# Two gate tiles of layer 0 are computed during the context's latent attention group instead of after it

## The chip, the cores and the metric

The kernel runs on one core of a Trainium2 chip. The metric is the device time of one execution in microseconds (us). Its engines are called by name here and by their short names in the profile: TensorE (PE, with PEld for its weight loads), VectorE (DVE), ScalarE (ACT), GpSimd (POOL) and SyncE (SP), which issues most DMAs. TensorE writes to eight PSUM banks; everything else lies in SBUF.

## The reference, cut to what matters

Two blocks with two layers each follow one another. The first is an image transformer block over 256 latent tokens and 256 context tokens of width 1024, the second a hybrid of retention, state space, stick-breaking and memory attention. The change lies in layer 0 of the first block. There, for the latent and for the context tokens:

```python
p = h @ w_in                       # h (tokens, 1024): normed and modulated input
gate_logits = p[..., :2048]        # two gates of 1024 columns
...
y_mla = dense_attention(mq, [mk_c, mk], [mv_c, mv])       # 8 heads, latent attention
y_na = neighborhood_attention(nq, nk, nv, nk_c, nv_c, rpb)  # 8 heads, with a bias
g = sigmoid(gate_logits)
y = g[..., :D_MODEL] * (y_mla @ w_mla_o) + g[..., D_MODEL:] * (y_na @ w_na_o)
x = x + gt1 * (y @ w_out)
```

In layer 0 the context tokens attend too (256 queries over 256 keys, without the bias); the latent tokens attend over 512 keys. All in float32.

## The kernel before

Activations lie transposed: 1024 features are eight k-steps of 128 partitions, and the 512 tokens (256 context, 256 latent) are columns. A product that must be exact to float32 is split: an operand is a high part (ScalarE copies it into a rounded type) and a low part (VectorE subtracts), and one k-step of a tile is three matmuls, high weight by high input, high by low, low by high (`split_product`, lines 562 to 565). A gate tile is 128 of the 1024 columns of the first gate for all 512 tokens: eight k-steps, 24 matmuls of 128x512. There are eight of them, called g1 0 to 7.

Weights come in chunks in the order of their use. A chunk of the large kind holds two gate tiles. It lands in one of three ring slots and is split into one of two buffers, `w_parts[0]` and `w_parts[1]`, in turn. `w_parts[1]` lies over the tensor `h`, where the low parts of the layer's input lie at first (`h_lo1`). Before it can be used, VectorE copies the low parts into `h_parts` (line 2315), eight copies, two a turn.

Attention runs in *turns*, one for each head and half of the queries: in layer 0 four groups of 16, `mla` (turns 0 to 15, latent queries, 512 keys), `mlac` (16 to 31, context queries, 256 keys: the context's latent group), `nac` (32 to 47, context, neighbourhood heads) and `na` (48 to 63, with the bias). Three engines walk through the same list, each at its own pace, and meet at semaphores:

- TensorE (`softmax_attention`, line 681) in turn i: the score product of turn i (line 906; in the last two groups those of turns i and i+1 together in even turns), the transposition of the probabilities of turn i-3 (line 715), a part of a value product of a unit of four turns, in odd turns (line 914), and then `fill(i)`, which is `gate_step` (line 931). Scores and transpositions share five banks in rotation, value products have one, gate tiles two.
- VectorE (`softmax`, line 1886) in turn i: the maximum of turn i's scores (line 1898; in `na` the bias before it), the reciprocal and the scaling for turn i-1 (lines 1902, 1904), every fourth turn the copy of a value product out of its bank (line 2299), and then `with_tile` (line 2301): the low-part copies in turns 32 to 35, and halves of weight splits (line 1941).
- ScalarE (`softmax`, line 1359) in turn i: the copy of the transposed probabilities of turn i-3 (line 1372), the exponential of turn i (line 1378), and then `split_gate` (line 1596): halves of weight splits (line 1423) and the exponential of a finished gate tile (line 1611).

Which turn does which gate work is set by constants. `gate_step` starts at turn `FILL_FROM[0]` = 34 and does two k-steps (6 matmuls) a turn, a tile in `FILL_STEPS[0]` = 4 turns: tiles 0 to 7 fill turns 34 to 65. `split_turn` (line 500) puts the halves of the four later weight chunks at turns 36, 37, then 44, 45, then 52, 53 and 60, 61 of ScalarE, and one turn later on VectorE. VectorE's first half waits for both of ScalarE's. The first chunk (tiles 0 and 1) is split in turns 4, 8, 11 and 13 of the first group. Behind the turns, TensorE goes on with the second gate and the output products (`turn_tile`), all of them split products.

Layer 1 has no context queries, two groups, and its own constants (18 and 2).

Of the kernel before, what the change touches and what calls it, by code (L numbers as in the profile page):

```python
# [41 lines left out]
KT = D // P  # L42
# [12 lines left out]
VALUES_AT = (2, 4, 7)  # L55
LINE = 128
TURN_BANKS, VALUE_BANKS, GATE_BANKS = (0, 1, 2, 3, 4), (5,), (6, 7)
FILL_FROM, FILL_STEPS = (34, 18), (4, 2)
GATES = [4, 5, 6, 7, 0, 1, 2, 3] + list(range(8, 16))
ADA = 24  # L60
FIRST = 8
# [198 lines left out]
def program(nc, dram, numbers):  # L260
# [3 lines left out]
    with ctx:  # L264
# [5 lines left out]
        def sem(name):  # L270
            if name not in sems:
                sems[name] = ctx.enter_context(nc.semaphore(name))
                count[name] = 0
            return sems[name]
# [9 lines left out]
        def event(name, *key):  # L284

            assert not numbers or (name, *key) in numbers, (name, *key)
            return sem(name), numbers.get((name, *key), 1)
# [20 lines left out]
        def given(ring_name, key):  # L308
            return rings[ring_name][numbers.get(("slot", ring_name, key), 0)]
# [46 lines left out]
        def part(name, shape, at):  # L356
            return nc.alloc_sbuf_tensor_at(name, shape, F32R, offset=at)
# [8 lines left out]
        h_lo1 = part("h_lo1", [P, KT, TT], h_at)  # L366
# [71 lines left out]
        at = 2048 + 8 * T  # L438
# [57 lines left out]
        def tile_index(l, g, u):  # L496

            return 16 * [t[0] for t in groups(l)].index(g[0]) + u

        def split_turn(l, i):  # L500


            out = []
            for c in range(1, 5):
                key = ("g1", l, 2 * c) if c < 4 else ("g2", l, 0)
                for a in range(2):
                    turn_of = FILL_FROM[l] + 2 * FILL_STEPS[l] * (c - 1) + 2 - l + a
                    if i == min(turn_of, 16 * len(groups(l)) - 1):
                        out.append((place[key][0], a))
            return out  # L510
# [5 lines left out]
        def groups(l):  # L516


            mla = lambda hd: (hd, slice(0, QK))
            na = lambda hd: (hd // 2, slice(ND * (hd % 2), ND * (hd % 2) + ND))  # L520
            out = [("mla", mq, mk, mv, mla, TC, 4, 0)]
            if l == 0:
                out.append(("mlac", mq, mk, mv, mla, 0, 2, 0))
                out.append(("nac", nq, nk, nv, na, 0, 2, 4))
            out.append(("na", nq, nk, nv, na, TC, 4, 4))
            return out
# [5 lines left out]
        def _(pe):  # L532
            used = {"chunk": -1, "open": set()}

            def next_bank(*key, until, among=None):

                return take(pe, "bank", key, until, among)

            def weights(*key):

                i, off, nk, w = place[key]
                if i != used["chunk"]:
                    used["chunk"] = i
                    pe.wait_ge(*event(loaded(i), i))
                used["open"].add(i)
                slot = (small if slots[i][0] > 1 else ring)[:, slots[i][1], :]
                return slot[:, off:off + nk * w].rearrange("p (k w) -> p k w", k=nk)

            def split_weights(key):

                i, off, nk, w = place[key]
                if i != used["chunk"]:
                    used["chunk"] = i
                    pe.wait_ge(*event("w_lo", i))
                used["open"].add(i)
                if slots[i][0] == 3:
                    both = small_hi[:, slots[i][3], :], small_lo[:, slots[i][1], :]
                else:
                    both = [w_parts[slots[i][3]][:, a, :] for a in range(2)]
                return [v[:, off:off + nk * w].rearrange("p (k w) -> p k w", k=nk) for v in both]  # L560

            def split_product(ps, w, k, hi, lo, nk):
                pe.matmul(ps, w[0][:, k, :], hi, start=k == 0, stop=False)  # L563
                pe.matmul(ps, w[0][:, k, :], lo, start=False, stop=False)  # L564
                return pe.matmul(ps, w[1][:, k, :], hi, start=False, stop=k == nk - 1)  # L565
# [12 lines left out]
            def full(ins, *key, more=False):  # L578

                ins.then_inc(*signal("psum_full", *key))  # L580
                for i in used["open"]:
                    seen[("chunk_used", i)] = ("psum_full", *key)
                if not more:
                    used["open"] = set()
# [8 lines left out]
            def linear(out, w, src, ready=None, first=True, last=True):  # L593

                nk = w.shape[1]
                for k in range(nk):
                    if ready:
                        pe.wait_ge(*event(*ready, k))
                    mm = pe.matmul(out, w[:, k, :], src(k), start=first and k == 0, stop=last and k == nk - 1)  # L599
                return mm  # L600
# [184 lines left out]
            for l in range(L):  # L785
                t0 = q0(l)
                cw = TT - t0
# [58 lines left out]
                for i in range(NH + 2):  # L846
                    if i < NH and i % 2 == 0:
                        ps = next_bank("mk", l, i // 2, until=("copied", "mk", l, i + 1))
                        mm = linear(ps[:, :], weights("uk", l, i // 2), lambda k: ckv[:, k, :], ("normed", "ckv", l))
# [20 lines left out]
                for i in range(NH):  # L870
                    if i < NH:
                        ps = next_bank("mq", l, i, until=("copied", "mq", l, i))
                        w = split_weights(("uq", l, i))
                        for k in range(6):
                            if i == 0:
                                pe.wait_ge(*event("cq_lo", l, k))
                            mm = split_product(ps[0:QK, 0:cw], w, k, cq_hi[k][:, t0:TT], cq_lo[:, k, t0:TT], 6)
# [42 lines left out]
                h_hi, h_lo = (h_parts[:, a, :, t0:TT] for a in range(2))  # L920
                gate_hi = h_hi1[:, :, t0:TT]
# [7 lines left out]
                gate_bank = [None]  # L929

                def gate_step(i):

                    n, step = divmod(i - FILL_FROM[l], FILL_STEPS[l])
                    if not 0 <= n < KT:
                        return
                    if step == 0:
                        gate_bank[0] = next_bank("g1", l, n, until=("gate_exp", "g1", l, n), among=GATE_BANKS)
                    w = split_weights(("g1", l, n))
                    at = KT // FILL_STEPS[l]
                    for k in range(at * step, at * step + at):  # L940
                        if n == 0:
                            pe.wait_ge(*event("h_lo", "h", l, k))
                        mm = split_product(gate_bank[0][:, 0:cw], w, k, gate_hi[:, k, :], h_lo[:, k, :], KT)
                    if step == FILL_STEPS[l] - 1:
                        full(mm, "g1", l, n)

                softmax_attention([t for g in groups(l) for t in head_tiles(*g[0:7])], 4, between=last_queries, fill=gate_step)
# [64 lines left out]
            for lw in range(L):  # L1012
                l = L + lw
# [20 lines left out]
                for name, *i in PROJ2[2:]:  # L1034
# [8 lines left out]
                    if (name, *i) == ("rk", 0):  # L1043
                        ps = next_bank("dt", l, until=("dt_bias", l, 1))
                        pe.wait_ge(*event("dt_row", l))
                        for t in range(2):
                            mm = pe.transpose(ps[:, 8 * t:8 * t + 8], dt_row[0:8, P * t:P * t + P], ident[0:8, 0:8])
# [9 lines left out]
                for t in range(2):  # L1057
                    ps = next_bank("xsT", l, t, until=("v_copied", "xs", l, 0, t))
                    for i in range(4):
                        pe.wait_ge(*event("xbc", l, i))  # L1060
                        mm = pe.transpose(ps[:, P * i:P * i + P], xbc[:, i, P * t:P * t + P], ident)
# [17 lines left out]
                for hd in range(8):  # L1079
# [6 lines left out]
                    if hd % 2 == 0:  # L1086
                        ps_y = next_bank("ssdY", l, hd // 2, until=("ssd_skip", l, hd // 2))
                    mm = causal_product(ps_y, vals2["xs"][:, :, 64 * hd:64 * hd + 64], given("tmp", ("ssd_g", l, hd)),
                                        slice(64 * (hd % 2), 64 * (hd % 2) + 64))
# [8 lines left out]
                for hd in range(4):  # L1098
# [10 lines left out]
                    mm = causal_product(ps, vals2["rv"][:, :, P * hd:P * hd + P], given("work", ("ret_decay", l, hd)))  # L1109
# [186 lines left out]
        def _(act):  # L1296
# [94 lines left out]
            l_now = [0]  # L1391
# [20 lines left out]
            def split_half(i, a):  # L1412

                _, slot, _, pair, before = slots[i]
                cols = slice(SLOT // 2 * a, SLOT // 2 * a + SLOT // 2)
                if a == 0:
                    split_next["at"] = i + 1
                    act.wait_ge(*event(loaded(i), i))
                    for j in before or []:
                        act.wait_ge(*event(*chunk_used(j)))  # L1420
                    if before is None:
                        act.wait_ge(*event("h_lo", "h", l_now[0], KT - 1))
                ins = act.activation(w_parts[pair][:, 0, cols], ring[:, slot, cols], ACT.Copy)
                if a:
                    ins.then_inc(*signal("w_hi", i))
# [6 lines left out]
            for l in range(L):  # L1432
                l_now[0] = l
                t0 = q0(l)
                cw = TT - t0
# [160 lines left out]
                def split_gate(g, u):  # L1596

                    if g[0] == "mla" and u == 0:
                        latent_values(3)
                    if g[0] == "mla" and u in (4, 8):  # L1600
                        split_half(place["g1", l, 0][0], u // 4 - 1)
                    for i, a in split_turn(l, tile_index(l, g, u)):
                        split_half(i, a)
                    n, at = divmod(tile_index(l, g, u) - FILL_FROM[l], FILL_STEPS[l])
                    if at == 0 and n > 0:
                        gate_exp1(n - 1)

                def gate_exp1(n):
# [86 lines left out]
            for lw in range(L):  # L1695
                l = L + lw
# [9 lines left out]
                for name, *i in PROJ2:  # L1706
                    i = i[0] if i else 0
# [1137 lines left out]
```

## Time and profile before

| | |
|---|---|
| runs, us | 2013.18, 2017.54, 2017.16; median 2017.16 |
| the profiled execution's own time, us | 2017.22 |
| its span (first to last instruction), us | 2015.3 |
| granted TensorE clock, mean | 0.986 |
| TensorE busy | 1912.1 us (95%) |
| VectorE busy | 1366.3 us (68%) |
| ScalarE busy | 922.4 us (46%) |
| chain that ended last | 73% TensorE, 12% VectorE, 8% ScalarE |
| turns 16 to 66 of layer 0 | about 279.5 to 391.3 us from the span's start |

A row of the timeline gives the start in us from the span's start, the duration, the engine, the line, and what is written from what; in brackets the idle time of the engine before it and what ended it. Matmuls are pipelined, so the recorded ends overlap the next start; the step from one start to the next is the time that an instruction costs. A row in which several instructions are merged has their count. A score product of 512 keys or a transposition is recorded in several passes (x2 or x4).

### The profile page before, as it was taken

What the parts mean: (1) busy time and instruction counts of PE and PEld (TensorE: products, weight loads), DVE (VectorE), ACT (ScalarE), POOL (GpSimd) and SP (SyncE); (2) the same over time, 40 slices, a digit from 0 to 9 for tenths busy, and PEclk for the clock granted to TensorE, in tenths of its full rate; (3) what the DMA queues carried; (4) which work ended last, traced back from release to release, by engine and by line L of the source; (5) the groups of instructions that cost most, each with busy time, mean ns of one, the idle gap of its engine ahead of it and who ended that gap; (6) DMA issues with size and microseconds to landing.
All of it is one profiled execution on the core that took longest, in us unless ns stands there. A gap on an engine that the chain in (4) does not pass through costs nothing.

```text
span 2015.3 us, 29593 instructions
## 1 busy us (share of the span) xinstructions
PE 1912.1 (95%) x11518; PEld 1604.6 (80%) x11518; DVE 1366.3 (68%) x2448; ACT 922.4 (46%) x1623; POOL 27.8 (1%) x56
## 2 busy tenths in 40 slices
PE   7999999999999999999999989999999989999987
PEld 3777456688888888887756888999999879999877
DVE  6665475688787887765567666665776755776764
ACT  3345465554433231354556655444444643544552
POOL 0000000000000000000000000000000000000000
PEclk9999999999999999999999999999999999999998
DMA  7331021255355555322131345454554325554323
GB/s 284 123 108 58 28 116 43 69 184 175 109 202 202 194 183 207 142 89 92 51 143 64 126 159 193 168 173 162 167 159 137 95 94 164 161 159 136 105 79 99
DMA packets 56473, 272.18 MB, mean 135 GB/s; under 512 B 6416, under 2 KB 7568, under 8 KB 39184
## 3 DMA queue, kind: packets, MB, share of 16 engines
q1 hardware_dynamic: 48848, 225.40, 32.7%
q0 software_dynamic: 7488, 44.90, 6.4%
q8 instruction: 93, 1.52, 0.3%
q14 instruction: 44, 0.36, 0.1%
HBM read 269.22 MB, written 1.05 MB: 134 GB/s over the span
## 4 chain that ended last, share of the span: by engine, by line
PE 73%; DVE 12%; ACT 8%; issue 5%; DMA 1%; SPq 0%; ACTq 0%; DVEq 0%
PE bank L563 18%; PE bank L565 17%; PE bank L564 17%; ACT w_parts L1409 3%; PE bank L906 2%; DVE small_lo L1928 2%; PE bank L914 2%; PE bank L599 2%; PE bank L715 2%; PE bank L1187 1%; PE bank L1188 1%; PE bank L1189 1%; PE bank L1003 1%; PE bank L610 1%; ACT small_hi L1407 1%
## 5 line engine op out<-in xcount | busy, mean ns | idle before, releaser
L563 PE MATMUL bank<-h_hi,small_hi 128*128 128x256 f32 (+3 forms) x992 | 312.5, 315 | 12.3 <-DVE small_lo L1928 6.2
L565 PE MATMUL bank<-h_hi,small_lo 128*128 128x256 f32 (+3 forms) x992 | 302.3, 305 | 0.0
L564 PE MATMUL bank<-h_lo,small_hi 128*128 128x256 f32 (+3 forms) x992 | 302.2, 305 | 0.0
L1928 DVE TENSOR_TENSOR small_lo<-ring,small_hi 128x1024 fp32r<-128x1024 f32 (+2 forms) x196 | 227.2, 1171 | 106.3 <-ACT small_hi L1407 104.6
L564 PE MATMUL bank<-h_parts,w_parts 128*128 128x256 f32 (+1 forms) x784 | 262.7, 335 | 0.0
L1931 DVE TENSOR_TENSOR w_parts<-ring,w_parts 128x2048 fp32r<-128x2048 f32 x87 | 199.3, 2291 | 90.0 <-ACT w_parts L1409 90.0
L1409 ACT ACTIVATE w_parts<-ring 128x2048 fp32r<-128x2048 f32 x86 | 164.0, 1907 | 174.4 <-PE bank L565 174.4
L563 PE MATMUL bank<-b_parts,w_parts 128*128 128x256 f32 (+1 forms) x656 | 218.8, 334 | 1.5 <-DVE w_parts L1931 1.1
L565 PE MATMUL bank<-b_parts,w_parts 128*128 128x256 f32 (+1 forms) x656 | 217.9, 332 | 0.0
L564 PE MATMUL bank<-b_parts,w_parts 128*128 128x256 f32 (+1 forms) x656 | 217.8, 332 | 0.0
L563 PEld LDWEIGHTS bank<-h_hi,small_hi 128*128 128x128 f32 (+2 forms) x992 | 188.3, 190 | 26.8 <-issue 13.9
L564 PEld LDWEIGHTS bank<-h_lo,small_hi 128*128 128x128 f32 (+2 forms) x992 | 188.4, 190 | 10.7 <-issue 2.2
L1407 ACT ACTIVATE small_hi<-ring 128x1024 fp32r<-128x1024 f32 (+2 forms) x196 | 193.6, 1006 | 6.7 <-DMA ring<-in_w 6.7
L565 PEld LDWEIGHTS bank<-h_hi,small_lo 128*128 128x128 f32 (+2 forms) x992 | 188.2, 190 | 8.7
L563 PE MATMUL bank<-h_parts,w_parts 128*128 128x256 f32 (+1 forms) x528 | 178.3, 338 | 9.8 <-DVE w_parts L1931 4.2
L565 PE MATMUL bank<-h_parts,w_parts 128*128 128x256 f32 (+1 forms) x528 | 176.1, 333 | 0.0
L564 PEld LDWEIGHTS bank<-h_parts,w_parts 128*128 128x128 f32 x784 | 150.5, 192 | 13.3
L563 PEld LDWEIGHTS bank<-b_parts,w_parts 128*128 128x128 f32 x656 | 124.5, 190 | 15.2 <-issue 3.1
L565 PEld LDWEIGHTS bank<-b_parts,w_parts 128*128 128x128 f32 x656 | 124.5, 190 | 12.0
L564 PEld LDWEIGHTS bank<-b_parts,w_parts 128*128 128x128 f32 x656 | 124.6, 190 | 11.8
L563 PEld LDWEIGHTS bank<-h_parts,w_parts 128*128 128x128 f32 x528 | 101.3, 192 | 22.1 <-issue 9.4
L1984 DVE SCALAR_TENSOR_TENSOR prob<-lowrank,c_rows 128x1024 f32<-128x1024 f32 x96 | 113.3, 1218 | 0.0
(297 smaller groups left out, 3836.6 us busy)
## 6 DMA issues: line engine op xcount, KB each, us to landing
ring<-in_w SPq DMA_DIRECT2D x204, 512.0 KB, 3.5
ring<-in_w SPq DMA_DIRECT2D x96, 1024.0 KB, 4.8
lowrank<-in_rows POOLq DMA_DIRECT2D x24, 1024.0 KB, 5.2
prob<-in_rows POOLq DMA_DIRECT2D x24, 512.0 KB, 3.8
wide<-in_ada SPq DMA_DIRECT2D x8, 1024.0 KB, 9.9
ring<-in_w SPq DMA_DIRECT2D x16, 288.0 KB, 2.9
lowrank<-in_bias POOLq DMA_DIRECT2D x2, 2048.0 KB, 11.2
x<-in_x SPq DMA_DIRECT2D x2, 1024.0 KB, 9.9
```

What stands on the lines that cost most here:

```text
L563: pe.matmul(ps, w[0][:, k, :], hi, start=k == 0, stop=False)
L564: pe.matmul(ps, w[0][:, k, :], lo, start=False, stop=False)
L565: return pe.matmul(ps, w[1][:, k, :], hi, start=False, stop=k == nk - 1)
L599: mm = pe.matmul(out, w[:, k, :], src(k), start=first and k == 0, stop=last and k == nk - 1)
L715: mm = pe.transpose(ps[:, P * k:P * k + P], given("prob", (g, u))[:, P * k:P * k + P], ident)
L906: return pe.matmul(ps[:, 0:P * nk], qs[r, a, q:q + P], ks[r, a, 0:P * nk], start=True, stop=True)
L914: mm = pe.matmul(ps[VD * a:VD * a + VD, 0:T], vs[:, k, v:v + VD], turned[:, a, k, :], start=k == 0, stop=k == nk - 1)
L1407: act.activation(small_hi[:, pair, 0:size], small[:, slot, 0:size], ACT.Copy).then_inc(*signal("w_hi", i))
L1409: act.activation(w_parts[pair][:, 0, 0:size], ring[:, slot, 0:size], ACT.Copy).then_inc(*signal("w_hi", i))
L1928: dve.tensor_tensor(small_lo[:, slot, 0:size], small[:, slot, 0:size], small_hi[:, pair, 0:size].bitcast(F32), ALU.subtract).then_inc(*sig ...
L1931: dve.tensor_tensor(w_parts[pair][:, 1, 0:size], ring[:, slot, 0:size], w_parts[pair][:, 0, 0:size].bitcast(F32), ALU.subtract).then_inc(* ...
L1984: ins = dve.scalar_tensor_tensor((product1 if l else product if b < 40 else product2)[:, s, :], w, 1.0, c_rows[:, s, :], ALU.mult, ALU.mul ...
```

## The change

Constants, and one new function `fill_at(l, i)` that says which tile and which step of it a turn does. In layer 0, turns 17 to 24 do tile 0 and turns 25 to 32 tile 1, one k-step (3 matmuls) a turn. `FILL_FROM[0]` becomes 31, and from it only tiles 2 to 7 are taken: turns 39 to 62, two k-steps a turn as before. Turns 33 to 38 and 63 to 65 do no gate work. Tiles 0 and 1 read the low parts in `h_lo1`, where they were first written, as the copies of turns 32 to 35 aren't there yet. So the second weight chunk, whose high half goes over them, waits on ScalarE for the end of tile 1 as well; its halves stay at turns 36 and 37, and those of the three chunks behind it come at 41, 42, then 49, 50 and 57, 58. The exponential of tile 0 comes in turn 25, that of tile 1 in turn 39, and those of the later tiles three turns earlier. Layer 1 keeps its turns.

```diff
--- before.py
+++ after.py
@@ -55,7 +55,7 @@
 VALUES_AT = (2, 4, 7)
 LINE = 128
 TURN_BANKS, VALUE_BANKS, GATE_BANKS = (0, 1, 2, 3, 4), (5,), (6, 7)
-FILL_FROM, FILL_STEPS = (34, 18), (4, 2)
+FILL_FROM, FILL_STEPS, EARLY = (31, 18), (4, 2), 17
 GATES = [4, 5, 6, 7, 0, 1, 2, 3] + list(range(8, 16))
 ADA = 24
 FIRST = 8
@@ -497,6 +497,14 @@
 
             return 16 * [t[0] for t in groups(l)].index(g[0]) + u
 
+        def fill_at(l, i):
+
+
+            if l == 0 and EARLY <= i < EARLY + 2 * KT:
+                return (*divmod(i - EARLY, KT), KT)
+            n, step = divmod(i - FILL_FROM[l], FILL_STEPS[l])
+            return (n, step, FILL_STEPS[l]) if (0 if l else 2) <= n < KT else (None, 0, 1)
+
         def split_turn(l, i):
 
 
@@ -504,7 +512,7 @@
             for c in range(1, 5):
                 key = ("g1", l, 2 * c) if c < 4 else ("g2", l, 0)
                 for a in range(2):
-                    turn_of = FILL_FROM[l] + 2 * FILL_STEPS[l] * (c - 1) + 2 - l + a
+                    turn_of = FILL_FROM[l] + 2 * FILL_STEPS[l] * (c - 1) + (5 if (l, c) == (0, 1) else 2 - l) + a
                     if i == min(turn_of, 16 * len(groups(l)) - 1):
                         out.append((place[key][0], a))
             return out
@@ -930,18 +938,19 @@
 
                 def gate_step(i):
 
-                    n, step = divmod(i - FILL_FROM[l], FILL_STEPS[l])
-                    if not 0 <= n < KT:
+                    n, step, steps = fill_at(l, i)
+                    if n is None:
                         return
                     if step == 0:
                         gate_bank[0] = next_bank("g1", l, n, until=("gate_exp", "g1", l, n), among=GATE_BANKS)
                     w = split_weights(("g1", l, n))
-                    at = KT // FILL_STEPS[l]
+                    early = l == 0 and n < 2
+                    at = KT // steps
                     for k in range(at * step, at * step + at):
-                        if n == 0:
+                        if n == (0 if l else 2):
                             pe.wait_ge(*event("h_lo", "h", l, k))
-                        mm = split_product(gate_bank[0][:, 0:cw], w, k, gate_hi[:, k, :], h_lo[:, k, :], KT)
-                    if step == FILL_STEPS[l] - 1:
+                        mm = split_product(gate_bank[0][:, 0:cw], w, k, gate_hi[:, k, :], (h_lo1 if early else h_lo)[:, k, :], KT)
+                    if step == steps - 1:
                         full(mm, "g1", l, n)
 
                 softmax_attention([t for g in groups(l) for t in head_tiles(*g[0:7])], 4, between=last_queries, fill=gate_step)
@@ -1420,6 +1429,8 @@
                         act.wait_ge(*event(*chunk_used(j)))
                     if before is None:
                         act.wait_ge(*event("h_lo", "h", l_now[0], KT - 1))
+                        if l_now[0] == 0:
+                            act.wait_ge(*event("psum_full", "g1", 0, 1))
                 ins = act.activation(w_parts[pair][:, 0, cols], ring[:, slot, cols], ACT.Copy)
                 if a:
                     ins.then_inc(*signal("w_hi", i))
@@ -1601,8 +1612,8 @@
                         split_half(place["g1", l, 0][0], u // 4 - 1)
                     for i, a in split_turn(l, tile_index(l, g, u)):
                         split_half(i, a)
-                    n, at = divmod(tile_index(l, g, u) - FILL_FROM[l], FILL_STEPS[l])
-                    if at == 0 and n > 0:
+                    n, step, _ = fill_at(l, tile_index(l, g, u))
+                    if n and step == 0:
                         gate_exp1(n - 1)
 
                 def gate_exp1(n):
```

## Rows read from the trace of the kernel before

**Rows 1.** Windows: us, busy of PE, PEld, DVE, ACT, POOL; clock, DMA, GB/s.

```profile
279.50:299.90 20.40, 18.89 (x116) 12.14 (x114) 14.38 (x53) 13.85 (x49) 0.00 (x0) 1.00 0.07 29
303.50:336.10 32.60, 32.60 (x164) 20.86 (x163) 18.81 (x55) 17.32 (x49) 0.00 (x0) 1.00 0.12 36
```

**Rows 2.** Who waited for whom, 279 to 303 us: total, times, longest.

```profile
PE bank L914 <- DVE tmp L2299: 1.5, 4, 0.4
```

**Rows 3.** Timeline of TensorE, end of the context group: start, us, instructions, idle before.

```profile
296.45 0.38 PE L715 MATMUL bank<-con,prob 128*128 128x128 f32 x2
296.76 0.65 PE L914 MATMUL bank<-probT,wide 128*64 128x256 f32 x4
297.34 0.70 PE L906 MATMUL bank<-wide 96*128 96x256 f32 x2
297.88 0.38 PE L715 MATMUL bank<-con,prob 128*128 128x128 f32 x2
298.10 0.60 PE L906 MATMUL bank<-wide 96*128 96x256 f32 x2
298.53 0.38 PE L715 MATMUL bank<-con,prob 128*128 128x128 f32 x2
299.35 0.65 PE L914 MATMUL bank<-probT,wide 128*64 128x256 f32 x4 [0.43 <-DVE tmp L2299]
299.93 0.70 PE L906 MATMUL bank<-wide 64*128 64x256 f32 x4
...
301.73 0.89 PE L906 MATMUL bank<-wide 64*128 64x256 f32 x4
```

**Rows 4.** Timeline of TensorE, filled turns 36 to 39.

```profile
307.47 0.70 PE L906 MATMUL bank<-wide 64*128 64x256 f32 x4
308.11 0.44 PE L715 MATMUL bank<-con,prob 128*128 128x128 f32 x2
308.30 0.48 PE L563 MATMUL bank<-h_hi,w_parts 128*128 128x512 f32 x1
...
310.67 0.50 PE L563 MATMUL bank<-h_hi,w_parts 128*128 128x512 f32 x1
311.00 0.39 PE L564 MATMUL bank<-h_parts,w_parts 128*128 128x512 f32 x1
...
311.93 0.40 PE L565 MATMUL bank<-h_hi,w_parts 128*128 128x512 f32 x1
312.25 0.70 PE L906 MATMUL bank<-wide 64*128 64x256 f32 x4
...
315.45 0.50 PE L563 MATMUL bank<-h_hi,w_parts 128*128 128x512 f32 x1
```

**Rows 5.** Timeline of VectorE: low-part copies, a maximum, weight halves, last scaling.

```profile
306.18 0.76 DVE L2315 CAST h_parts<-h_lo 128x512 fp32r<-128x512 f32 x2
308.20 0.42 DVE L1898 TENSOR_REDUCE stat<-bank 128x1 f32<-128x256 f32 x1 [1.27 <-PE bank L906]
...
312.07 1.23 DVE L1941 TENSOR_TENSOR w_parts<-ring,w_parts 128x1024 fp32r<-128x1024 f32 x1 [2.07 <-ACT w_parts L1423]
...
314.34 1.22 DVE L1941 TENSOR_TENSOR w_parts<-ring,w_parts 128x1024 fp32r<-128x1024 f32 x1
...
383.93 0.49 DVE L1904 TENSOR_SCALAR prob<-prob,stat 128x512 f32<-128x512 f32 x1
```

**Rows 6.** Timeline of ScalarE: the exponential of turn 36.

```profile
308.86 0.47 ACT L1378 ACTIVATE prob<-bank,stat 128x256 f32<-128x256 f32 x1
```

**Rows 7.** Timeline of TensorE: turn 65's fill and the last transposition.

```profile
386.57 0.50 PE L563 MATMUL bank<-h_hi,w_parts 128*128 128x512 f32 x1
...
388.06 0.60 PE L715 MATMUL bank<-con,prob 128*128 128x128 f32 x4
```

**Rows 8.** Timeline of TensorE, and the window, behind the gap of 542 us.

```profile
542.05 0.47 PE L563 MATMUL bank<-h_parts,w_parts 128*128 128x512 f32 x1 [2.68 <-DVE w_parts L1931]
...
542.10:545.60 3.50, 3.50 (x9) 2.78 (x10) 3.50 (x7) 1.43 (x3) 0.52 (x1) 0.55 0.76 253
```


## The prediction

> **What bounds the kernel now.** I read the busy time by stage first. In the context latent group (turns 16 to 31) TensorE is busy 18.89 of 20.40 us; in the context neighbourhood group, where each turn carries two of the eight k-steps of a gate tile, 32.60 of 32.60; VectorE and ScalarE are at 58% and 53% there [rows 1]. So from turn 34 to the end of the turns the time is TensorE's own work, and a matmul moved out of it only pays if it lands in a place where TensorE waits.
>
> How much waiting is there in the place it moves to? The table of waits gives four waits of 1.5 us in all, each for the copy that frees the single value bank [rows 2]. In the timeline a transposition and the value product behind it start 0.82 us apart with such a wait (298.53, 299.35), and 0.31 without (296.45, 296.76). So 0.51 us by the starts, every fourth turn, one of the four shorter: 1.8 us in all; everything else between these rows is back to back [rows 3]. 48 matmuls of about 0.23 us are to go there, 11 us of work into 1.8 us of holes. Almost all of it must be paid for by what is left out later, and that is the question.
>
> **The change part by part.** The number of matmuls, of splits, of copies and of DMAs stays the same. Tiles 0 and 1 leave turns 34 to 41 and go to turns 17 to 32, one k-step (3 matmuls) a turn. Tiles 2 to 7 move three turns ahead, to turns 39 to 62. Turns 33 to 38 and 63 to 66 then carry no gate work.
>
> *1. The small fills of turns 17 to 31.* The filled turns of now price a fill [rows 4]: behind a value product the first matmul takes 0.33 us (310.67 to 311.00), one in the middle 0.23, and the last one ahead of a score product 0.32 (311.93 to 312.25); behind a transposition it starts 0.19 us after it. A fill of six costs 1.49 us on the mean of its two places: a filled pair of turns is 4.78 us from scores to scores (307.47 to 312.25), the unfilled pair 1.80 (299.93 to 301.73) [rows 3, 4]; (4.78 - 1.80)/2 = 1.49. For three matmuls in an odd turn I get 0.33 + 0.23 + 0.33 = 0.89. In an even turn a score product would now stand behind a matmul fill instead of a transposition, and takes 0.53 instead of 0.43 us (297.34 to 297.88 against 298.10 to 298.53), so 0.19 + 0.87 + 0.53 less the 0.22 + 0.43 of now = 0.93 or 0.94. Eight odd and seven even turns: 8 x 0.89 + 7 x 0.93 = 13.6 us. The waits for the value bank go, as the turn gets 0.9 us longer and VectorE's copy is then early: -1.8. Sum **+11.8**. Bounds: the large fill has an overhead of 1.49 - 6 x 0.23 = 0.11 over its bare matmuls; with that a turn costs 0.80 and the sum is 10.2. Nothing excludes 1.0 a turn, 13.2. I take 0.91, built from the same neighbours. (That the waiting inside the short products might be covered too, and a turn cost far less, is rival B.)
>
> *2. From the scores of turn 32 to the first step of tile 2 in turn 39.* Before, TensorE needs 315.45 - 299.93 = 15.52 us for this and does five large fills in it (turns 34 to 38). After, its own work is the small fill of turn 32 (0.75), and otherwise 1.80 a pair: 0.75 + 4 x 1.80 = 7.9 us. But tile 2 needs the split halves of its weights, and these stay bound to turns 36 and 37 on ScalarE and 37 and 38 on VectorE. I follow that chain from a, the start of turn 32's scores. VectorE is without a pause from there in the rows of before (the two halves of the last pair of low-part copies start at 306.18 and end at 306.94: a + 7.0) and stays so, since its own work, not TensorE, sets it: the scores of turns 34 to 36 are there in time. Then the maximum of turn 36, 0.42 (the row at 308.20), and 0.09 to ScalarE's exponential: a + 7.5. From that exponential to the end of the low half is 314.34 + 1.22 - 308.86 = 6.7 us in the rows of before, all ScalarE and VectorE: two halves on ScalarE one turn apart, VectorE idle 2.07 us for the second, then its own two halves at 312.07 and 314.34 with a softmax turn between [rows 5, 6]. None of it waits for TensorE, so it keeps its length. **a + 14.2**: the fill of turn 39 starts 1.3 us earlier than before and not 7.6: 14.2 - 7.9 = 6.3 us of TensorE standing still that the large fills cover now. Behind VectorE's wait stand the maxima of turns 38 and 39 and the copy that frees the value bank, so the stand comes in pieces: before the transposition of turn 38, before the value product of turn 39 (the longest), before the fill itself. Sum **-1.3**. The bounds: 7.9 (nothing waits) gives -7.6; 15 us (TensorE delays the chain after all) gives -0.5.
>
> *3. Turns 39 to 62.* 24 large fills as before, at the same price. Three more chunks are split three turns earlier, at odd and even turns changed over; at most some 0.4 us either way in the waits near them. 0.
>
> *4. The end.* Fills in turns 63, 64 and 65 go; the last one takes 388.06 - 386.57 = 1.49 us [rows 7]: -4.5. What is late next? The last probabilities are scaled at 383.93 and transposed at 388.06, 4.1 us later, and in turns 61 and 62 VectorE has two weight halves of 1.14 us each less to do after the change [rows 5, 7]; so they are there when three fills are missing, to within 0.1. Sum **-4.4**. Bounds: -4.5 and, if each of the three transpositions waits 0.5 us, -3.
>
> *5. The clock.* Where TensorE idled 2.68 us ahead of a row of 512-column matmuls (at 542.05), the granted clock was 0.55 of full in the 3.5 us behind it: that is the 1.2 GHz level for nearly all of it, and 9 matmuls started in them [rows 8], which take 9 x 0.23 = 2.1 us at full clock. So such a drop costs about 1.4 us where the matmuls are dense, and less where TensorE waits anyway. In part 2 TensorE would stand for most of the last 6 us, with short products between. I expect one drop, ended partly within the stand: **+1.2**, bounds 0 and +2.8 (two). The Trainium skill (TensorE: Matmul & The Clock Gate, the section on why this matters for your kernels) warns of idle gaps between bursts of matmuls because the engine falls back to half rate; in this kernel the row agrees, and by the rule alone this change, which opens such a gap where there is none, is a loss in itself.
>
> The sum: 11.8 - 1.3 + 0 - 4.4 + 1.2 = **+7.3 us**. The wait added on ScalarE in turn 36 (tile 1 complete, turn 32) costs nothing: the exponential of turn 36 ahead of it in the queue needs scores that TensorE issues four turns after tile 1; were it late, both halves, the following exponentials and all of part 2 would be. The exponential of gate tile 0 (0.6 us, now in turn 25) is hidden in ScalarE's idle third [rows 1]. Reading the low parts at their first place costs nothing: same size, same engine. The DMA issues only move with the splits that free their slots, at 36 GB/s in this stretch [rows 1].
>
> The profiled execution took 2017.22 us, of which 2015.3 are the span; the median of the three runs is 2017.16. So both give **2024.5 us**. What follows the turns is TensorE-bound again and gets everything equally late.
>
> **The rivals.**
> *A, a small loss or none.* The small fills cost their lower bound (-1.6) and the clock doesn't fall (-1.2): +4.5, 2021.7; with the clock drop 2022.9; with a shorter chain in part 2 by 1 to 2 us some +3, 2020. For it: the even fill's overhead is only 0.11. Against: the single score turns have more changes of operand per turn.
> *B, faster: small fills hide in the context group.* Its score products are two passes of 256 columns and take 0.43 to 0.53 us, while a pass in the paired group takes 0.16 (four from 307.47 to 308.11) [rows 3, 4]. If these 0.2 us a product are latency that a fill covers, together with that of the transposition and of the value product, a small fill costs 0.2 instead of 0.91: 15 x 0.71 = 10.7 less, so -3.4 with the clock drop and -4.6 without: 2013.8 or 2012.6. It turns the sign from a price under 0.42 (0.91 - 7.3/15), and gives more than 0.2% from one under 0.16 to 0.24. The Trainium skill (TensorE: Matmul & The Clock Gate, What happens when you issue a matmul) says that the engine pulls weight loads ahead of running matmuls, which is this rival's mechanism: long matmuls would hide the loads of the short ones. Against: in the filled turns of now that cover is there too, and the fill still costs more than its matmuls, not less [rows 4].
> *C, the stand does not come*, because the chain in part 2 is quicker when TensorE is: up to -6.3 and no clock drop, 2017.0. Against: rows 5 and 6 show VectorE waiting for ScalarE, not for TensorE.
> *D, worse:* two drops of the clock, or the chain late by 1.5 us more: 2027.
> That the change doesn't do what it says would show as fills in turns 34 to 38; the loop excludes it.
>
> **How the numbers follow.** Forecast (2022.5 to 2026.5) 0.58, A 0.18, C 0.08, B 0.07, D 0.09. 0.2% is 4.0 us, about what this kernel's measurement can tell, so slower begins at 2021.2: the forecast, D and a third of A give slower 0.73; the rest of A and C, with a share of noise, same 0.18; faster 0.09. Range 2018 to 2027.
>
> **What would show it.** TensorE idle of 5 to 7 us between the last small fill and tile 2's first matmul, with releasers VectorE's value copy and its weight half (L1941); the mean step of a context turn at 1.9 to 2.0 us (now 1.17, waits and all); no wait for the value bank in turns 19 to 31; the three last transpositions close together; one clock row below 1 near turn 39. A step under 1.6 us there, or an idle under 2 us at turn 39, would make the prediction wrong.

## The result, and the profile after

Over 18 runs of each, the changed kernel takes 2020.53 us (median, 2016.85 to 2025.88), the kernel before 2015.79 (2011.31 to 2019.65). The ratio is 1.0031, 95% interval 1.0022 to 1.0040: slower by 0.3%, some 6 us. The forecast was +7.3 us on 2017.2. Single runs scatter by several us, more than most steps below are worth, and the granted clock goes along with it: of the 85 runs of the kernel before that were timed beside the experiments, those at a mean clock of 0.986 took 2017.3 us on average, those at 0.989 took 2011.7; a straight line through all of them gives 1.8 us for a thousandth of clock. So I use a second measure, taken inside one profiled execution: the **stage**, from the scores of turn 16 to the first matmul of g2. It was 391.27 - 279.49 = 111.78 us and is 395.18 - 278.18 = 117.00: +5.2 us. Each kernel was profiled once, so the stage has no interval. Where two kernels do the same work it repeats closely: from the first wait for the value bank to the wait of turn 34 it is 18.91 us in the kernel before and 18.89 in b1_before_halves. A fall of the clock inside the stage may not come in every execution.

The small fills, timeline of TensorE of the changed kernel, two turns of the context group:

```profile
296.95 0.60 PE L914 MATMUL bank<-wide 96*128 96x256 f32 x2
297.38 0.38 PE L723 MATMUL bank<-con,prob 128*128 128x128 f32 x2
297.52 0.48 PE L571 MATMUL bank<-h_hi,w_parts 128*128 128x512 f32 x1
...
298.07 0.40 PE L573 MATMUL bank<-h_hi,w_parts 128*128 128x512 f32 x1
298.30 0.60 PE L914 MATMUL bank<-wide 96*128 96x256 f32 x2
298.74 0.38 PE L723 MATMUL bank<-con,prob 128*128 128x128 f32 x2
...
299.63 0.50 PE L571 MATMUL bank<-h_hi,w_parts 128*128 128x512 f32 x1
...
300.19 0.40 PE L573 MATMUL bank<-h_hi,w_parts 128*128 128x512 f32 x1
300.43 0.60 PE L914 MATMUL bank<-wide 96*128 96x256 f32 x2
```

A pair of turns takes 3.48 us (296.95 to 300.43). Before it took 2.59 with its wait of 0.51 and 2.08 without [rows 3]. So a small fill costs 0.70 us, and no wait for the value bank is left in turns 19 to 31. The rows show why it is not 0.91: the fill starts 0.14 us behind the transposition (not 0.19), its last matmul takes 0.23 ahead of the scores (not 0.32, [rows 4]), and the scores behind a fill take 0.43 or 0.44, in the even turns too, where they took 0.53 behind the value product. From turn 16's scores to turn 32's it is 29.30 us (278.18 to 307.48) against 20.44: +8.9.

The empty turns, TensorE again, from turn 32's scores to those of turn 40:

```profile
307.48 0.70 PE L914 MATMUL bank<-wide 64*128 64x256 f32 x4
...
310.91 0.63 PE L723 MATMUL bank<-con,prob 128*128 128x128 f32 x4 [0.22 <-ACT prob L1387]
312.41 0.65 PE L922 MATMUL bank<-probT,wide 128*64 128x256 f32 x4 [0.88 <-DVE tmp L2310]
...
314.16 0.63 PE L723 MATMUL bank<-con,prob 128*128 128x128 f32 x4 [0.47 <-ACT prob L1387]
...
317.30 0.67 PE L723 MATMUL bank<-con,prob 128*128 128x128 f32 x4 [1.07 <-ACT prob L1387]
320.54 0.97 PE L922 MATMUL bank<-probT,wide 128*64 128x256 f32 x4 [2.57 <-DVE tmp L2310]
321.72 0.77 PE L571 MATMUL bank<-h_hi,w_parts 128*128 128x512 f32 x1 [0.21 <-issue]
...
324.39 0.70 PE L914 MATMUL bank<-wide 64*128 64x256 f32 x4
```

Tile 2 starts at 321.72, 14.24 us behind turn 32's scores (307.48). The bracketed idle adds up to 5.4 us, the largest piece 2.57 for the copy out of the value bank. What VectorE and ScalarE did in that time:

```profile
313.73 0.76 DVE L2326 CAST h_parts<-h_lo 128x512 fp32r<-128x512 f32 x2
314.40 0.42 DVE L1909 TENSOR_REDUCE stat<-bank 128x1 f32<-128x256 f32 x1
...
318.13 1.23 DVE L1952 TENSOR_TENSOR w_parts<-ring,w_parts 128x1024 fp32r<-128x1024 f32 x1 [2.06 <-ACT w_parts L1434]
...
320.07 0.42 DVE L2310 COPY tmp<-bank 128x256 f32<-128x256 f32 x1
320.40 1.22 DVE L1952 TENSOR_TENSOR w_parts<-ring,w_parts 128x1024 fp32r<-128x1024 f32 x1
```

```profile
314.91 0.47 ACT L1387 ACTIVATE prob<-bank,stat 128x256 f32<-128x256 f32 x1
...
315.38 1.04 ACT L1434 ACTIVATE w_parts<-ring 128x1024 fp32r<-128x1024 f32 x1
...
317.04 1.06 ACT L1434 ACTIVATE w_parts<-ring 128x1024 fp32r<-128x1024 f32 x1
```

The chain stands as it did in rows 5 and 6, copy by copy: the last two low-part copies from 313.73, the maximum of turn 36 at 314.40, its exponential at 314.91 (7.43 behind turn 32's scores), ScalarE's two halves at 315.38 and 317.04, VectorE idle 2.06 us for the second, the value copy caught behind VectorE's first half and a softmax turn at 320.07, and the second half ending at 321.62, 6.7 us after the exponential. TensorE's fill starts 0.1 later. Then the clock, two windows of 3.3 us (columns as in rows 1):

```profile
317.60:320.90 3.30, 0.73 (x7) 0.33 (x6) 2.73 (x6) 1.61 (x5) 0.00 (x0) 0.98 0.02 5
320.90:324.20 3.30, 3.09 (x10) 1.82 (x6) 1.48 (x4) 1.05 (x3) 0.00 (x0) 0.51 0.42 129
```

In the first TensorE was busy 0.73 us of 3.30; in the second the clock is at 0.51, the 1.2 GHz level, and turn 39's fill from 321.72 to 324.39 takes 2.67 us, where such a fill took 1.58 (310.67 to 312.25, [rows 4]): +1.1.

Later turns, and the end:

```profile
356.19 0.63 PE L723 MATMUL bank<-con,prob 128*128 128x128 f32 x4 [0.89 <-ACT prob L1387]
...
380.38 0.63 PE L723 MATMUL bank<-con,prob 128*128 128x128 f32 x4 [0.27 <-ACT prob L1387]
...
385.36 1.13 PE L914 MATMUL bank<-wide 64*128 64x512 f32 x4
...
393.30 1.95 PE L922 MATMUL bank<-probT,wide 128*64 128x256 f32 x16 [0.73 <-issue]
...
395.18 0.50 PE L571 MATMUL bank<-h_hi,w_parts 128*128 128x512 f32 x1
```

The waits of 0.89 and 0.27 us in turns 52 and 60 are new; one of 0.37 in turn 55 went. What made the first of them, on VectorE and ScalarE:

```profile
352.88 1.22 DVE L1952 TENSOR_TENSOR w_parts<-ring,w_parts 128x1024 fp32r<-128x1024 f32 x1 [0.92 <-ACT w_parts L1434]
```

```profile
355.27 0.69 ACT L1387 ACTIVATE prob<-bank,stat 128x512 f32<-128x512 f32 x1 [1.93 <-DVE stat L1909]
```

VectorE waits 0.92 us for ScalarE's second half, the maximum of turn 51 stands behind that, ScalarE's exponential waits 1.93 us for it, and TensorE's transposition at 356.19 waits for the exponential. From the scores of turn 62 to g2 it is 9.82 us (385.36 to 395.18); before 14.06: -4.2.

### The profile page after: what moved, and what is told of

The parts are those of the page before. It is cut to its first block, busy times and chain, and to the rows that moved or that the text cites. A ratio compares the mean times of both kernels' runs of the same rounds, so it can differ in the third digit from the quotient of the medians.

```text
span 2017.9 us, 29593 instructions
## 1 busy us (share of the span) xinstructions
PE 1910.4 (95%) x11518; PEld 1603.4 (79%) x11518; DVE 1366.6 (68%) x2448; ACT 923.0 (46%) x1623; POOL 27.8 (1%) x56
## 4 chain that ended last, share of the span: by engine, by line
PE 72%; DVE 12%; ACT 8%; issue 5%; DMA 2%; SPq 0%; ACTq 0%; DVEq 0%
PE bank L571 17%; PE bank L573 17%; PE bank L572 17%; ACT w_parts L1418 3%; PE bank L914 2%; DVE small_lo L1939 2%; PE bank L922 2%; PE bank L607 2%; PE bank L723 2%; DMA wide<-in_ada 1%; PE bank L1196 1%; PE bank L1198 1%; PE bank L1197 1%; PE bank L1012 1%; PE bank L618 1%
## 5 line engine op out<-in xcount | busy, mean ns | idle before, releaser
L572 PE MATMUL bank<-h_parts,w_parts 128*128 128x256 f32 (+1 forms) x768 | 256.4, 334 | 0.0
L571 PE MATMUL bank<-h_parts,w_parts 128*128 128x256 f32 (+1 forms) x528 | 178.5, 338 | 9.8 <-DVE w_parts L1942 4.2
L573 PE MATMUL bank<-h_parts,w_parts 128*128 128x256 f32 (+1 forms) x528 | 175.9, 333 | 0.0
L572 PEld LDWEIGHTS bank<-b_parts,w_parts 128*128 128x128 f32 x656 | 124.6, 190 | 11.8
```

## The experiments

All were timed in five rounds beside the kernel before. Every ratio is to that kernel.

**e1_halves** tells the chain apart from the softmax's own pace. Its edit, on the changed kernel:

```diff
@@ split_half, ScalarE, layer 0's chunks
+                elif i <= place["g2", 0, 0][0]:
+                    ins.then_inc(*signal("w_half", i))
@@ split_half, VectorE
-                    dve.wait_ge(*event("w_hi", i))
+                    dve.wait_ge(*event("w_half" ... else "w_hi", i))
+                else:
+                    dve.wait_ge(*event("w_hi", i))
```

> The changed kernel, but in layer 0 VectorE's first half of a weight split waits for ScalarE's first half alone, not for both. Stage time is the time from the scores of turn 16 to the first matmul of g2 (before 111.78 us, after 116.99). Theory (the stand of TensorE in turns 34 to 39 is the chain of the split halves): VectorE no longer idles 2.06 us, the low half is ready about 1.7 us earlier, the small waits near the three other chunks (0.8 us) go too: stage 114.2 to 115.3 us, 2 to 2.8 us off the changed kernel's time (about 2018). Rival (the stand is set by the softmax's own latency or by the fallen clock): stage 116.5 to 117.2, no change.

Stage 114.44 us, ratio 1.0006 (0.9994 to 1.0018). The two halves on VectorE, and TensorE:

```profile
316.68 1.23 DVE L1956 TENSOR_TENSOR w_parts<-ring,w_parts 128x1024 fp32r<-128x1024 f32 x1 [0.39 <-ACT w_parts L1434]
318.95 1.22 DVE L1956 TENSOR_TENSOR w_parts<-ring,w_parts 128x1024 fp32r<-128x1024 f32 x1
```

```profile
307.71 0.70 PE L914 MATMUL bank<-wide 64*128 64x256 f32 x4
...
317.52 0.63 PE L723 MATMUL bank<-con,prob 128*128 128x128 f32 x4 [1.07 <-ACT prob L1387]
319.09 0.65 PE L922 MATMUL bank<-probT,wide 128*64 128x256 f32 x4 [0.94 <-DVE tmp L2314]
320.27 0.77 PE L571 MATMUL bank<-h_hi,w_parts 128*128 128x512 f32 x1 [0.53 <-issue]
```

As expected. VectorE waits 0.39 us instead of 2.06, the value product of turn 39 waits 0.94 instead of 2.57, and tile 2 starts 12.56 us behind turn 32's scores (307.71, 320.27) instead of 14.24. The wait in turn 38 (1.07) is unchanged, since it is for an exponential that stands behind ScalarE's first half. The chain is the cause of what it moved, 1.7 us. The 4.1 us of idle that are left between turn 32's scores and tile 2 are put down to the rest of the chain by the rows alone.

**b1_before_halves**, the same edit on the kernel before:

> The kernel before with the same finer waits as e1_halves. There the chain runs beside large fills: both theories expect no change beyond the 0.4 us wait near turn 55 (stage 111.2 to 111.8 us, 2015.5 to 2016). If it gains 2 us or more, the split waits cost the kernel before too, and e1's gain says nothing on the stand.

Stage 111.32 us, ratio 0.9998 (0.9987 to 1.0010), as expected. Where large fills stand beside it the finer waits are worth 0.46 us; e1 gained 2.56, 1.68 of them in the empty turns.

**e2_one_tile** takes half of the early work back and covers turns 35 to 38 with it:

```diff
-            if l == 0 and EARLY <= i < EARLY + 2 * KT:
+            if l == 0 and EARLY <= i < EARLY + KT:
-            return (n, step, FILL_STEPS[l]) if (0 if l else 2) <= n < KT else (None, 0, 1)
+            return (n, step, FILL_STEPS[l]) if (0 if l else 1) <= n < KT else (None, 0, 1)
...
-                    early = l == 0 and n < 2
+                    early = l == 0 and n < 1
...
-                            act.wait_ge(*event("psum_full", "g1", 0, 1))
+                            act.wait_ge(*event("psum_full", "g1", 0, 0))
```

> The changed kernel, but only tile 0 goes ahead (turns 17 to 24, one k-step a turn); tile 1 is done in turns 35 to 38, two k-steps a turn, with the copied low parts; tiles 2 to 7 stay at 39 to 62. Theory (what costs is the stretch without cover behind which the weight chain stands): the stand of 6.3 us and the clock drop go, 8 small fills cost 8 x 0.70 = 5.6 less 0.8 of waits, 4 large fills go (6.0): stage 111 to 112.5 us, level with the kernel before (2015 to 2016.5). Rival (small fills in the context group are what costs, half of them left): stage 114 to 115, 2018.

Stage 114.44 us, ratio 1.0010 (0.9999 to 1.0022). Both numbers missed; 114.44 is the rival's. Half of the early fills do cost what they should (turn 16's scores to turn 32's: 25.23 us, 8 x 0.70 less 0.8 of waits above 20.44). What the theory had not counted on shows in these rows:

```profile
304.45 0.70 PE L914 MATMUL bank<-wide 64*128 64x256 f32 x4
...
307.88 0.63 PE L723 MATMUL bank<-con,prob 128*128 128x128 f32 x4 [0.73 <-ACT prob L1387]
309.38 0.65 PE L922 MATMUL bank<-probT,wide 128*64 128x256 f32 x4 [0.88 <-DVE tmp L2310]
...
321.31 0.47 PE L571 MATMUL bank<-h_hi,w_parts 128*128 128x512 f32 x1 [0.21 <-DVE w_parts L1952]
```

```profile
309.90:313.30 3.40, 3.40 (x12) 1.97 (x10) 1.52 (x6) 1.05 (x3) 0.00 (x0) 0.59 0.00 0
313.40:316.80 3.40, 3.40 (x18) 2.38 (x17) 1.70 (x6) 2.62 (x8) 0.00 (x0) 0.92 0.00 0
```

The long stand of turns 38 and 39 is gone (0.21 left), but at turn 34, which I had left empty, TensorE waits 0.73 us, as in the kernel before (303.36, in its trace), and then 0.88 in turn 35, which is new there. The clock fell right behind these two short waits (0.59): 12 instructions against 18 in equal stretches.

**e3_late** leaves tiles 2 to 7 where they were:

```diff
-FILL_FROM, FILL_STEPS, EARLY = (31, 18), (4, 2), 17
+FILL_FROM, FILL_STEPS, EARLY = (34, 18), (4, 2), 17
...
-... + (5 if (l, c) == (0, 1) else 2 - l) + a
+... + (2 - l) + a
```

> The changed kernel, but tiles 2 to 7 and the splits behind the second chunk stay where they were (turns 42 to 65), so turns 33 to 41 are empty and 63 to 65 full. Theory (TensorE is held by VectorE's waiting in turns 38 and 39 whatever it is asked to do next): the fill of turn 42 starts about 17.4 us after the scores of turn 32, stage 115.4 to 116.8 us, at most 1.5 less than the changed kernel (2019 to 2020.5). Rival (the stand comes from asking for tile 2 three turns earlier): the stand of 6.3 us goes, the three fills at the end come back at 4.3: stage 113.5 to 114, 2017.5.

Stage 116.91 us, 0.1 above the range, ratio 1.0023 (1.0013 to 1.0034):

```profile
307.20 0.70 PE L914 MATMUL bank<-wide 64*128 64x256 f32 x4
...
320.26 1.12 PE L922 MATMUL bank<-probT,wide 128*64 128x256 f32 x4 [2.61 <-DVE tmp L2310]
...
326.06 0.57 PE L571 MATMUL bank<-h_hi,w_parts 128*128 128x512 f32 x1
```

Turn 39's value product waits 2.61 us although nobody asks for tile 2 before turn 42, whose fill starts at 326.06, 18.86 behind turn 32's scores. That is 1.5 later than I had it, as the granted clock was 0.50 from 320 to 326 us here. The rival, that asking three turns early makes the stand, is out.

**f0_cover34** puts tile 1 into turns 34 to 38. **f2_odd** and **g1_even** then move tile 0's small fills to odd or even turns; **f1_odd_halves** and **g2_even_halves** add e1's edit.

The edits in short:

```diff
@@ f0, on e2
+            if l == 0 and 34 <= i < 39:
+                return 1, i - 34, 5
...
+                    some = [range(0, 2), range(2, 4), range(4, 6), range(6, 7), range(7, 8)][step] if steps == 5 else ...
@@ f2, on f0
+FILL_FROM, FILL_STEPS, EARLY = (31, 18), (4, 2), 19
...
+            if l == 0 and i % 2 and EARLY <= i < EARLY + 2 * KT:
+                return 0, (i - EARLY) // 2, KT
@@ g1, on f2
+FILL_FROM, FILL_STEPS, EARLY = (31, 18), (4, 2), 18
...
+            if l == 0 and i % 2 == 0 and EARLY <= i < EARLY + 2 * KT:
```

> As e2_one_tile, but tile 1 lies in turns 34 to 38 (2, 2, 2, 1 and 1 k-steps) instead of 35 to 38. e2 still had waits of 0.73 and 0.88 us in turns 34 and 35, a clock drop right behind them (its fills of turns 35 and 36 ran at half rate) and a stage of 114.44 us. Theory (turn 34 too needs its cover; the clock falls because of the short gaps there): no wait for the value copy in turn 35, no drop near turn 35, stage 111.3 to 112.3 us, level with the kernel before. Rival (e2's loss is in the small fills of the context group): stage 114.2 or more, as e2.

Stage 113.33 us, ratio 1.0009 (1.0001 to 1.0018). No wait in turn 35 and no drop, as expected; but the stage is 1 to 2 us above what I had and 0.9 below the rival's. 1.5 us of waits stand in turn 39 (value copy, weight half), where turns 37 and 38 hold half a fill each:

```profile
323.21 0.65 PE L924 MATMUL bank<-probT,wide 128*64 128x256 f32 x4 [0.93 <-DVE tmp L2313]
324.44 0.47 PE L573 MATMUL bank<-h_hi,w_parts 128*128 128x512 f32 x1 [0.57 <-DVE w_parts L1955]
```

The waits in turns 52 and 60 (0.87, 0.27) are there as well.

> As f0_cover34, but tile 0's eight small fills stand in the odd turns 19, 21, ... 33 instead of in 17 to 24. Theory (a small fill costs 0.70 us less what it covers): all four waits for the value copy go (1.8 us against 0.8 in f0) and so does most of the wait of 1 us in turn 34: stage 109.8 to 110.8 us, 1 to 2 under the kernel before. Rival (VectorE's copy follows TensorE, so that a fill only moves the wait): stage as f0.

Stage 113.66 us, ratio 1.0001 (0.9993 to 1.0010). The rival holds: all four waits for the value copy stay. The wait of 0.73 us in turn 34 did go, but tile 2 starts 15.78 us behind turn 32's scores as in f0, so that gave nothing. TensorE and VectorE:

```profile
285.74 0.60 PE L916 MATMUL bank<-wide 96*128 96x256 f32 x2
286.17 0.38 PE L725 MATMUL bank<-con,prob 128*128 128x128 f32 x2
286.99 0.65 PE L924 MATMUL bank<-probT,wide 128*64 128x256 f32 x4 [0.44 <-DVE tmp L2313]
287.57 0.50 PE L573 MATMUL bank<-h_hi,w_parts 128*128 128x512 f32 x1
```

```profile
285.71 0.42 DVE L1912 TENSOR_REDUCE stat<-bank 128x1 f32<-128x256 f32 x1 [1.53 <-PE bank L916]
...
286.51 0.42 DVE L2313 COPY tmp<-bank 128x256 f32<-128x256 f32 x1
```

VectorE's copy (286.51) follows its maximum of turn 22 (285.71). Between turn 22's scores and the value product of turn 23 (286.99) stand only turn 23's scores (285.74) and two transpositions; the fill comes behind the product (287.57) and moves both alike.

> f2_odd with the finer waits of e1_halves (VectorE's first half of a split waits for ScalarE's first half alone, layer 0). Theory: 0.8 to 1.2 us less than f2 from the waits near the four chunks, stage 108.5 to 109.8 us, 2 to 3 under the kernel before's 111.78, and a time of 2013 to 2014.5, 0.10 to 0.15% under it. Rival: no less than f2.

Stage 111.54 us, ratio 1.0000 (0.9990 to 1.0011). The stage is 2 us above the expected range, since f2 was. Against f2 it gains 2.1, twice what I expected: the waits of 0.93, 0.87 and 0.27 us in turns 39, 52 and 60 are all gone.

> f2_odd with tile 0's eight small fills in the even turns 18, 20, ... 32 instead of the odd ones. f2 kept all its waits of 0.43 us for the value copy: it stands on VectorE behind the maximum of the even turn's scores, and an odd turn's fill lies behind the value product, so it moves both. Theory: an even turn's fill lies between those scores and the value product and covers the copy; the four waits go: stage 113.66 less 1.6 to 2.0, 111.6 to 112.1 us. Rival (the copy is late for another reason, and every turn must be filled to hide it): stage 113.4 to 113.8.

Stage 111.62 us, ratio 1.0009 (1.0001 to 1.0018). The four waits are gone, 2.0 us, as expected. The time doesn't bear this out: by its stage the ratio should be 0.9999, and against f2, which was timed in another set of rounds, it should have fallen by 0.0010 and rose by 0.0008. The runs' mean granted clock was lower, 0.9866 against 0.9874 in the kernel before beside it. At 1.8 us for a thousandth this makes 1.4 of the 2 us that are missing (an estimate).

> f1_odd_halves (stage 111.54 us) with the small fills in the even turns. Theory: stage 109.5 to 110.0 us, 1.8 to 2.3 under the kernel before's 111.78; time 2012.5 to 2014.5, a ratio near 0.999. Rival: stage 111.3 to 111.7, as f1.

Stage 109.51 us, ratio **0.9983 (0.9974 to 0.9992)**, 2011.56 us against 2014.21, 1 us under the range: this version is faster than the kernel before by 0.17%. Its stage, in the range, gives 2.3 us of that. It is also below the changed kernel, by their two ratios. Two waits are left between turns 16 and 65:

```profile
307.54 0.41 PE L725 MATMUL bank<-con,prob 128*128 128x128 f32 x2 [0.22 <-ACT prob L1390]
...
318.99 0.47 PE L573 MATMUL bank<-h_hi,w_parts 128*128 128x512 f32 x1 [0.57 <-DVE w_parts L1959]
```

## Why the prediction was right

Step by step, forecast and measured (us in the profiled execution):

| step | forecast | measured |
|---|---|---|
| small fills, turns 16 to 31 | +11.8 | +8.9 |
| turn 32 to tile 2's start in turn 39 | -1.3 | -1.3 |
| turns 39 to 62 without the clock | 0 | +0.8 |
| the clock | +1.2 | +1.1 (in the profile) |
| the end | -4.4 | -4.2 |
| sum | +7.3 | +5.2 (the time: +4.4 to +8.1 by the ratio) |

The main step was right to the tenth: the weight chain doesn't shorten when TensorE gets quicker, so tile 2 starts 14.2 us behind turn 32's scores, with 5.4 us of idle between (6.3 forecast). e1 and b1 show that the chain makes 1.7 us of it, e3 that tile 2's early place doesn't make it, and e2 and f0 that large fills beside the chain hide most of it. Rival C (no stand) is refuted.

*The term that was mis-sized is the small fill: 0.91 forecast, 0.70 measured.* Fifteen of them are 3.1 us. I had built it from the neighbours of a six-matmul fill in the paired group. And I had counted one joint twice: the first product behind a value product takes 0.1 us more, whether it is a score product (0.53) or a fill's first matmul (0.33), and I had charged the fill for it and left it with the scores. The lower bound, 0.80, was too high as well. So a context turn takes 1.75 us on the mean of turns 24 to 31 (293.47 to 307.48), below the 1.9 to 2.0 that I had named as the sign, though above the 1.6 that would have refuted it. Rival B has the direction: 0.70 is just the three matmuls at 0.23, so a fill adds no overhead, but none of the matmuls' own time is hidden, and 0.70 is far from its 0.2.

Step 3 had the waits too low: with the splits at turns 49, 50 and 57, 58 the maximum of an odd turn stands behind VectorE's wait for a half, and the exponential and the transposition behind the maximum. I had bounded this by 0.4, and it cost 1.16 less the 0.37 saved. e1, where VectorE doesn't wait for the second half, removes both waits.

The clock fell where it was put, in e1's profile too (once) and in e3's (for about twice as long). Of the executions without a profile the mean granted clock is on record, and not where it fell: 0.9857 over the 18 runs of the changed kernel and the same over e3's 12, against 0.9874 over the 85 of the kernel before. At 1.8 us for a thousandth that is some 3 us (an estimate), more than the 1.1 of the one profile. e1 and e2, with one drop each in their profiles, have 0.9873 and 0.9874, so how often it falls stays open. The Trainium skill (TensorE: Matmul & The Clock Gate, why this matters for your kernels) warns of idle gaps between bursts of matmuls. The rows agree in that the clock was at 0.51 behind the idle of 2.57 us.

That the time came within 1 us of the forecast is in part luck. The small fills were 2.9 us cheaper than forecast, the later waits 0.8 dearer, and the rest of the difference between stage (+5.2) and time (+6.3) lies in the runs' clock or in the noise, which isn't settled. The median itself, 2020.53, lies below the 2022.5 to 2026.5 that I held likeliest: the three runs that I started from put the kernel before at 2017.16, 18 runs at 2015.79, and the medians differ by only 4.7.

Without the idle of the empty turns and the drop the change would have had 5.2 - 5.4 - 1.1 = -1.3 us, an estimate; or -0.6, if it keeps the 0.73 us of idle that the kernel before has in turn 34. g2, with nearly everything covered and the finer waits, which are worth 0.46 to the kernel before, measured -2.3.

## What to carry to other kernels

Work that rides beside a slower engine's chain is cover. Before moving it, follow that chain from engine to engine in the rows, with the waits of one helper for another in it: what keeps its length when the covering engine gets quicker will be stood through in full. And a filler helped with a wait only where it stood between the instruction that releases the chain and the one that waits (even turns here), not somewhere near.

## What the runs showed of the hardware

In e2_one_tile TensorE's clock fell to half (0.50 from 311 to 313 us) right behind two idles of 0.73 and 0.88 us with 0.6 us of transpositions between; the kernel before and f0 had the 0.73 alone in the same place, the changed kernel 0.22 and 0.88, and all three kept 1.00 there. Each is one profile. And a fill of three 512-column matmuls between short ones cost 0.70 us, its matmuls' bare time: the score products beside it (two passes of 256 columns, 0.43 to 0.53 us) don't get dearer by it.
